# Gate and up projections of a feed-forward as seven products of half-size blocks

## What is computed

```python
def swiglu(x, w_in, w_out):
    g, u = jnp.split(x @ w_in, 2, axis=-1)
    return (jax.nn.silu(g) * u) @ w_out
...
        f = swiglu(rms_norm(h, norm_pre_ffn[layer]), w_ffn_in[layer], w_ffn_out[layer])
        h = h + rms_norm(f, norm_post_ffn[layer])
```

## Time and profile before

| | us |
|---|---|
| median of 3 runs | 1938.16 |
| span of the profiled execution | 1936.8 |
| TensorE busy | 1895.3 |
| VectorE busy | 1025.4 |
| ACT busy | 774.5 |
| last feed-forward after its first four tiles, to L1466 | 341.4 |

### The profile page before, as it was taken

One profiled execution on the slowest core, in us unless ns is written; L12 is line 12 of the kernel. 1 busy time (PEld: TensorE's weight loads), 2 busy tenths in 40 slices (PEclk: granted clock), 3 DMA queues, 4 the chain that ended last, 5 costly groups with the idle time before them and its releaser, 6 DMA issues.

```text
span 1936.8 us, 28778 instructions
## 1 busy us (share of the span) xinstructions
PE 1895.3 (98%) x11544; PEld 1664.7 (86%) x11544; DVE 1025.4 (53%) x1465; ACT 774.5 (40%) x1259; POOL 32.2 (2%) x31
## 2 busy tenths in 40 slices
PE   7999999999999999999999999999999999999997
PEld 7888789999999999888888877787899888888886
DVE  4654475654444455544444467778547463333335
ACT  5355443433222345423232434635675442212232
POOL 0100000100000000000000000000000000000000
PEclk9999999999999999999999999999999999999998
DMA  5111101232222222322222222222103122232221
GB/s 190 68 66 45 58 1 57 87 103 88 95 91 88 92 95 88 109 98 92 93 98 98 91 95 87 76 76 77 55 1 116 70 98 90 86 101 103 89 92 50
DMA packets 47187, 162.36 MB, mean 84 GB/s; under 512 B 5368, under 2 KB 7672, under 8 KB 46936
## 3 DMA queue, kind: packets, MB, share of 16 engines
q1 hardware_dynamic: 46208, 158.60, 23.8%
q10 hardware_dynamic: 856, 2.00, 0.3%
HBM read 156.38 MB, written 4.19 MB: 83 GB/s over the span
## 4 chain that ended last, share of the span: by engine, by line
PE 94%; DVE 3%; ACT 2%; DVEq 1%; issue 1%; DMA 0%; SPq 0%; ACTq 0%
PE ps L468 80%; PE ps L1048 2%; PE ps L919 1%; PE ps L589 1%; PE ps L1068 1%; PE ps L895 1%; PE ps L897 1%; PE ps L1053 0%; PE ps L992 0%; PE ps L564 0%; DVE wlo L2364 0%; ACT WU L2065 0%; PE ps L565 0%; PE ps L1180 0%; PE ps L1209 0%
## 5 line engine op out<-in xcount | busy, mean ns | idle before, releaser
L468 PE MATMUL ps<-UH,whi 128*128 128x264 f32 (+2 forms) x1904 | 646.2, 339 | 13.5 <-DVE wlo L2364 10.2
L468 PE MATMUL ps<-UL,whi 128*128 128x264 f32 (+2 forms) x1904 | 637.6, 335 | 0.0
L468 PE MATMUL ps<-UH,wlo 128*128 128x264 f32 (+3 forms) x1616 | 522.0, 323 | 0.0
L1529 ACT ACTIVATE whi<-raw 128x1024 fp32r<-128x1024 f32 x282 | 295.7, 1052 | 436.3 <-PE ps L468 415.5
L468 PEld LDWEIGHTS ps<-UH,whi 128*128 128x128 f32 x1904 | 358.6, 188 | 55.3 <-issue 13.6
L468 PEld LDWEIGHTS ps<-UL,whi 128*128 128x128 f32 x1904 | 358.6, 188 | 39.5 <-issue 2.4
L2364 DVE TENSOR_TENSOR wlo<-raw,whi 128x1024 fp32r<-128x1024 f32 x248 | 308.3, 1246 | 48.7 <-ACT whi L1529 37.0
L468 PEld LDWEIGHTS ps<-UH,wlo 128*128 128x128 f32 (+1 forms) x1616 | 303.8, 188 | 24.6
L468 PE MATMUL ps<-HH,whi 128*128 128x264 f32 (+1 forms) x768 | 246.4, 321 | 0.0
L468 PE MATMUL ps<-HL,whi 128*128 128x264 f32 (+1 forms) x768 | 246.3, 321 | 0.0
L468 PE MATMUL ps<-HH,wlo 128*128 128x264 f32 (+1 forms) x768 | 245.7, 320 | 0.0
(11 more groups left out here) (466 smaller groups left out, 2358.5 us busy)
## 6 DMA issues: line engine op xcount, KB each, us to landing
raw<-W SPq DMA_DIRECT2D x284, 512.0 KB, 3.2
H<-xT SPq DMA_DIRECT2D x4, 528.0 KB, 7.3
spill<-H SPq DMA_DIRECT2D x1, 2048.0 KB, 9.0
H<-spill SPq DMA_DIRECT2D x1, 2048.0 KB, 8.6
MEM<-memT ACTq DMA_DIRECT2D x1, 1024.0 KB, 4.7
out<-H SPq DMA_DIRECT2D x2, 512.0 KB, 3.0
out<-H SPq DMA_DIRECT2D x4, 256.0 KB, 3.1
masks<-masks SPq DMA_DIRECT2D x1, 768.0 KB, 10.1
```

Source lines behind the costliest of these rows:

```text
L468: mm = pe.matmul(dst, a, b, start=start and n == 0, stop=stop_ and n == 2)
L1529: act.activation(whi[s % NB][:, :, :], raw[s % NB][:, :, :], ACT.Copy).then_inc(w_hi, 1)
```

## The change

Of the 22 pairs, 4 stay as they are (PLAIN) and 18 are computed by seven products instead of eight (the Winograd form of Strassen's scheme). A pair is seen as a 2 x 2 matrix of weight blocks (gate or up by the first or second four of the 8 feature blocks) times a 2 x 2 matrix of token blocks (the same two groups of four by tokens 0 to 255 or 256 to 511). Each product has 4 blocks, three passes and 256 tokens.

- *Token parts.* Seven combinations of the normed input, each 4 x 256 per partition, are made once: VectorE scales the tokens by gain and norm factor (`tokens`, XQ), makes four sums, ACT rounds (`tokens_hi`, TH), VectorE subtracts (`tokens_lo`, TL). So gate and up tiles of these pairs carry the norm's factor.
- *Weight parts.* Four sums of weight blocks per pair are made by VectorE (`pair_sums`, PS), then rounded and subtracted like a slot. A pair has four slots: three of 8 blocks, one of 4.
- *Accumulators.* Bank x collects b11, t2, t3, t4; ACT copies it after b11, after t2 and after t3 (`shot`, snap), and bank z after t1, before b22 is added to it; y holds b21. VectorE builds gate and up halves from banks and copies. Pairs take banks 4, 5, 6 and 7, 1, 3 in turn.
- *Down projection.* Instead of two rounds of 11 groups: four chunks of 4 groups, each in four pieces of two tiles (`down(c, q)`), two pieces before pair 0 and one behind each of pairs 0, 1 and 4 to 15, and a last round of 6 groups. Each is added to FO in memory.
- *Plain pairs* 2 and 3 go to banks 4, 5, 0 and 2, the first of them behind r_ready 7.
- *SP* loads the two slots of a pair as one DMA of 1 MB (`refill_pair`), a down slot as one of 512 KB (`refill_down`).

TensorE:

```diff
+            def plain(bank, *free):
+                pe.wait_ge(*free)
+                for k in range(KT):
+                    wh, wl = take()
+                    mm = passes(ps[:, bank, :], wh, wl, UH[:, k, META:L], UL[:, k, META:L], k == 0, k == KT - 1)
+                mm.then_inc(tile_done, 1)
...
+            def product(bank, v, half, t, first):
+                for k in range(4):
+                    mm = passes(ps[:, bank, 0:NMEM], whi[v % NB][:, 4 * half + k, :], wlo[v % NB][:, 4 * half + k, :],
+                                TH[:, t, k, :], TL[:, t, k, :], first and k == 0, k == 3, True)
+                mm.then_inc(AFTER["pair"][0], 1)
...
+                if i >= 2:
+                    pe.wait_ge(*later("pair_out", 4 * (i - 2) + 4))
+                pe.wait_ge(w_lo, v + 1)
+                turned_in(1)
+                product(x, v, 0, b11, True)
+                turned_in(2)
+                product(y, v, 1, b21, True)
+                pe.wait_ge(w_lo, v + 2)
+                turned_in(4)
+                pe.wait_ge(*later("snap", 4 * i + 1))
+                product(x, v + 1, 0, t2, False)
+                turned_in(5)
+                product(z, v + 1, 1, t1, True)
+                pe.wait_ge(w_lo, v + 3)
+                turned_in(6)
+                pe.wait_ge(*later("snap", 4 * i + 2))
+                product(x, v + 2, 0, t3, False)
+                pe.wait_ge(*later("snap", 4 * i + 3))
+                product(z, v + 2, 1, b22, False)
+                pe.wait_ge(w_lo, v + 4)
+                turned_in(7)
+                pe.wait_ge(*later("snap", 4 * i + 4))
+                product(x, v + 3, 0, t4, False)
+            first = TILE0["ffn"]
+            plain(4, r_ready, 7)
+            plain(5, r_ready, 7)
+            plain(0, evac[0], first // 2 + 1 + FREE)
+            plain(2, evac[1], first // 2 + 1 + FREE)
+            down(0, 0, EARLY_SLOT)
+            down(0, 1, EARLY_SLOT + 1)
+            for i in range(PAIRS):
+                pair(i)
+                if i in DOWN_AFTER:
+                    down(*DOWN_AFTER[i], DOWN_AT[i])
```

ACT, the start and a pair (next_hi is the down slot's high part first, where there is one, then the next pair's):

```diff
+            def shot(i, n, bank, done, kept):
+                act.wait_ge(*later("pair", 7 * i + done))
+                if i:
+                    act.wait_ge(*later("pair_out", 4 * (i - 1) + kept))
+                act.activation(snap[:, n, :], ps[:, bank, 0:NMEM], ACT.Copy).then_inc(AFTER["snap"][0], 1)
+            plain_silu(0)
+            plain_silu(1)
+            weights_hi(0, to=FFN_SLOT + 7)
+            f_hi(0)
+            weights_hi(0, to=FFN_SLOT + 8)
+            f_hi(1)
+            tokens_hi(b11, 0, 1)
+            plain_silu(2)
+            tokens_hi(t1, 0, 2)
+            weights_hi(0, to=FFN_SLOT + 9)
+            tokens_hi(b21, 2, 3)
+            tokens_hi(b22, 3, 3)
+            f_hi(2)
+            weights_hi(0, to=FFN_SLOT + 10)
+            tokens_hi(t3, 1, 4)
+            plain_silu(3)
+            pair_hi(0, 0)
+            f_hi(3)
+            tokens_hi(t2, 3, 5)
+            tokens_hi(t4, 2, 6)
+            for q in range(1, 4):
+                pair_hi(0, q)
...
+                shot(i, 0, x, 1, 1)
+                next_hi(i, 0)
+                shot(i, 1, x, 3, 3)
+                shot(i, 2, z, 4, 2)
+                next_hi(i, 1)
+                shot(i, 3, x, 5, 2)
+                next_hi(i, 2)
+                act.wait_ge(*later("pair_out", 4 * i + 3))
+                act.activation(GA[i % 2][:, :], GA[i % 2][:, :], ACT.Silu).then_inc(N["f_silu"], 1)
+                next_hi(i, 3)
+                f_hi(PLAIN + i)
+                if i in DOWN_AFTER:
+                    next_hi(i, 4)
```

VectorE, from the first gate to pair 0, then a pair, then the half evictions of the end (`tokens` is one instruction of 512 elements, `tokens_lo` one of 1024):

```diff
+            gate(0, first, 0)
+            gate(1, first + 2, 1)
+            gated_up(0, first + 1, 2)
+            gated_up(1, first + 3, 3)
+            weights_lo(0, to=FFN_SLOT + 7)
+            weights_lo(0, to=FFN_SLOT + 8)
+            f_lo(0)
+            f_lo(1)
+            for k in range(4):
+                x = tokens(k)
+            x.then_inc(AFTER["t_x"][0], 1)
+            gate(2, first + 4, 4)
+            tokens_lo(b11, 0, 1)
+            dve.drain()
+            dve.tensor_tensor(XQ[:, 0, :, :], XQ[:, 0, :, :], XQ[:, 1, :, :], ALU.subtract).then_inc(AFTER["t_x"][0], 1)
+            for k in range(4, KT):
+                x = tokens(k)
+            x.then_inc(AFTER["t_x"][0], 1)
+            gated_up(2, first + 5, 5)
+            dve.drain()
+            dve.tensor_tensor(XQ[:, 1, :, :], XQ[:, 3, :, :], XQ[:, 1, :, :], ALU.subtract).then_inc(AFTER["t_x"][0], 1)
+            weights_lo(0, to=FFN_SLOT + 9)
+            tokens_lo(b21, 2, 3)
+            tokens_lo(b22, 3, 4)
+            gate(3, first + 6, 0)
+            weights_lo(0, to=FFN_SLOT + 10)
+            f_lo(2)
+            gated_up(3, first + 7, 2)
+            dve.drain()
+            dve.scalar_tensor_tensor(XQ[:, 3, :, :], XQ[:, 3, :, :], -1.0, XQ[:, 0, :, :], ALU.mult, ALU.subtract
+                                     ).then_inc(AFTER["t_x"][0], 1)
+            f_lo(3)
+            dve.scalar_tensor_tensor(XQ[:, 2, :, :], XQ[:, 3, :, :], -1.0, XQ[:, 2, :, :], ALU.mult, ALU.subtract
+                                     ).then_inc(AFTER["t_x"][0], 1)
+            down_out(0, 0)
+            pair_sums(0)
+            down_out(0, 1)
+            pair_lo(0, 0)
+            tokens_lo(t2, 3, 6)
+            down_out(0, 2)
+            tokens_lo(t1, 0, 2)
+            pair_lo(0, 1)
+            down_out(0, 3)
+            tokens_lo(t3, 1, 5)
+            pair_lo(0, 2)
+            tokens_lo(t4, 2, 7)
+            pair_lo(0, 3)
...
+                dve.wait_ge(*later("pair", 7 * i + 2))
+                dve.wait_ge(*later("snap", 4 * i + 1))
+                dve.tensor_tensor(a[:, 0:NMEM], ps[:, y, 0:NMEM], snap[:, 0, :], ALU.add).then_inc(AFTER["pair_out"][0], 1)
+                if i in DOWN_AFTER:
+                    down_lo(i)
+                if i + 1 < PAIRS:
+                    pair_sums(i + 1)
+                next_lo(i, 0)
+                dve.wait_ge(*later("snap", 4 * i + 4))
+                dve.tensor_tensor(c[:, NMEM:SEQ], snap[:, 3, :], snap[:, 2, :], ALU.add).then_inc(AFTER["pair_out"][0], 1)
+                dve.wait_ge(*later("pair", 7 * i + 6))
+                dve.tensor_tensor(a[:, NMEM:SEQ], ps[:, z, 0:NMEM], snap[:, 1, :], ALU.add).then_inc(AFTER["pair_out"][0], 1)
+                next_lo(i, 1)
+                dve.wait_ge(*later("pair", 7 * i + 7))
+                dve.wait_ge(N["f_silu"], j + 1)
+                dve.scalar_tensor_tensor(c[:, 0:NMEM], ps[:, x, 0:NMEM], -1.0, a[:, 0:NMEM], ALU.mult, ALU.mult
+                                         ).then_inc(AFTER["pair_out"][0], 1)
+                dve.drain()
+                dve.scalar_tensor_tensor(c[:, NMEM:SEQ], c[:, NMEM:SEQ], -1.0, a[:, NMEM:SEQ], ALU.mult, ALU.mult
+                                         ).then_inc(AFTER["f_c"][0], 1)
+                next_lo(i, 2)
+                if i in DOWN_AFTER:
+                    down_out(DOWN_AFTER[i][0], 2 * DOWN_AFTER[i][1])
+                f_lo(j)
+                if i in DOWN_AFTER:
+                    down_out(DOWN_AFTER[i][0], 2 * DOWN_AFTER[i][1] + 1)
+                next_lo(i, 3)
...
             def evict_half(x, e):
-                a = GA[e][:, part(x)]
+                o = FO[:, KT - 2 + e, x * NMEM:(x + 1) * NMEM]
                 dve.wait_ge(tile_done, t + 2 * x + e + 1)
-                dve.drain()
-                dve.tensor_tensor(a, ps[:, 2 * ((t + e) % 2) + x, 0:NMEM], R[0][:, part(x)], ALU.mult)
-                dve.drain()
-                o = FO[:, KT - 2 + e, part(x)]
-                dve.tensor_tensor(o, o, a, ALU.add).then_inc(h_final, 1)
+                dve.tensor_tensor(o, o, ps[:, 2 * ((t + e) % 2) + x, 0:NMEM], ALU.add).then_inc(h_final, 1)
```

SP:

```diff
+            def refill_pair(i, ready):
+                s = PAIR_SLOT + 2 * i
+                sp.wait_ge(w_lo, ready)
+                sp.dma_start(raw_p[i % 2][:, :, :].rearrange("p (a s) e -> p a (s e)", a=2),
+                             W[s:s + 2].rearrange("a p s e -> p a (s e)")).then_inc(AFTER["pair_in%d" % (i % 2)][0], 16)
...
+            for i in range(PAIRS):
+                if i + 2 < PAIRS:
+                    refill_pair(i + 2, PAIR_AT[i] + 4)
...
+                if i in DOWN_AFTER and i != DOWN_ORDER[-1]:
+                    sp.wait_ge(w_lo, DOWN_AT[i] + 1)
+                    refill_down(DOWN_ORDER.index(i) + 1)
```

More of the change, by code:

```diff
@@ L94 @@
 END_OF = tile_ends()
-assert len(END_OF) == _t and END_OF[-1] == NBLOCKS
+assert len(END_OF) == _t and END_OF[-1] <= NBLOCKS
 def last_tile(slot):
@@ new lines, in down @@
+            def down(c, q, v):
+                pe.wait_ge(w_lo, v + 1)
+                for x in range(2):
+                    t = DOWN_TILE + KT * c + 2 * q + x
+                    pe.wait_ge(evac[t % 2], t // 2 + FREE)
+                    for k in range(CHUNK):
+                        f = CHUNK * c + k
+                        if q == 0 and x == 0:
```

(4 more changed lines are left out.)

350 lines of the change are left out of this document (256 added, 94 removed).

## The result

The changed kernel takes 1908.6 us (median of 4 executions: 1906.97, 1907.21, 1909.99 and 1916.27), the kernel before on the same chip 1938.19 us (4 executions, 1937.76 to 1938.74). The profiled execution is the slowest of the four, 1916.27 us with a span of 1914.5 us. That one lies on the forecast of 1916.4; the other three do not. So there are two questions: did each step come as forecast in the profiled execution, and what do the other three have that it has not.

A forecast was written before the change was run, and what follows sets the result against it. TensorE was taken to bound the kernel. Matmuls -19.1, start gap -2.5, clock -1.7, stalls +2.6 and tail -1.0 sum to -21.7 us, from the median 1938.16 to 1916.4 us; range 1912 to 1923.

The forecast's parts named there:

- What bounds the kernel: Whole kernel: TensorE, busy 98% of the span, sets the time; only matmul time or a TensorE stall can be won.
- Part 1: Eighteen gate/up pairs: seven half-width products replace eight, at 0.118 us per narrow matmul; L1466 is reached 19.1 us earlier.
- the low end: Bottom of the forecast range, 1912 us: no stall at all and 0.117 us per narrow matmul.
- the walk: The three engines' instruction lists laid side by side in order, priced with trace durations, to find when TensorE must wait.
- Part 2: Start of the last feed-forward: the 2.35 us bank-wait gap goes, 2.5 us won, and its half clock, 1.7 us.
- Part 3: ACT and VectorE readiness: 2.6 us of stalls, 2.1 at block 3 of the first down piece, 0.5 in the pairs.
- Part 4: Tail behind L1466: two half evictions on the chain become an add alone, 0.5 us each, 1.0 us won.
- 1, the stall halves the clock: Rival: the new 2.1 us stall at the start halves the clock behind it, 1.7 us more, 1918.1 us; chance 0.22.
- 2, VectorE behind all through: Rival: VectorE durations 10% longer in start and bare pairs, 4.8 us more stall, 1921.2 us; chance 0.15.
- 3, snapshots: Rival: TensorE waits in every pair for ACT's accumulator copies, making the kernel slower than before; chance 0.05.
- 4, narrow matmuls not at half the time: Rival: narrow matmuls take 0.1325 us, so seven products win nothing, about 1938 us; chance 0.03.

The follow-up runs named there:

- eight: Changed kernel with the product of b21 made twice in each of the 18 pairs, 12 narrow matmuls more per pair; 1939.93 us, ratio 1.0006.
- gap: Changed kernel with the first plain tile waiting again for the eviction of an early tile, as before the change; 1916.36 us, ratio 0.9875.
- again2: Changed kernel run once more without any edit, to see how its executions spread; 1912.15 us, ratio 0.9873.
- again: Changed kernel run once more, unmodified, beside the first variants; 1917.89 us, ratio 0.9891.
- again3: Changed kernel run unmodified on the same chip as the last variant, for comparison; 1912.48 us, ratio 0.986.
- restart: Changed kernel with TensorE waiting ahead of each down piece behind a pair until VectorE has built that pair's last tile, 14 times; 1946.31 us, ratio 1.0039.
- kick: Changed kernel with one extra matmul of 130 tokens, result unused, in front of the second product of pair 9; 1913.42 us, ratio 0.9868.
- kickall: Changed kernel with f_lo(3) ahead of the token sum and an extra 130-token matmul in all 18 pairs; 1911.02 us, ratio 0.9862.
- best: Changed kernel with f_lo(3) ahead of the token sum and an extra 130-token matmul in pairs 0 and 4 only; 1909.45 us, ratio 0.9851.
- flo: Changed kernel with the low part f_lo(3) moved ahead of the token sum that stood before it; 1910.18 us, ratio 0.9861.
- flo2: Second run, without further edit, of the changed kernel with f_lo(3) ahead of the token sum; 1910.53 us, ratio 0.9864.
- kicksizes: Changed kernel with one extra matmul in each of pairs 4 to 13, of lengths from 64 to 256 tokens; 1910.81 us in one execution.

## Why the prediction was right and wrong

**What bounds the kernel**: right. 216 narrow matmuls more made the span 25.0 us longer (**eight**), and a gap of 0.93 us of idle 1.2 us longer (**gap**).

**Part 1, seven for eight, -19.1 us**: the failed step. The count is right, the price of the narrow matmul is not: 0.118 us was taken as its one price, and the pairs ran at 0.1178 us in some executions and at 0.1134 in others. "I take 0.2318 and 0.118 (the second from the tail [...])" took one price for the narrow matmul from two stretches that happened to have it, and the low end went to 0.117 only. The trace of the kernel before had a third stretch of narrow matmuls, in the projection of the mixer, where they start 0.113 us apart. Its timeline on TensorE:

```profile
1486.58 0.28 PE L468 MATMUL ps<-YH,whi 128*128 128x256 f32 x1
...
1489.41 0.28 PE L468 MATMUL ps<-YL,whi 128*128 128x256 f32 x1
```

From the first to the last row 25 matmuls later it is 2.83 us. I did not look there. (This stretch is at 0.1136 us in all 14 traces, whatever the pace of the pairs: it shows the lower price, not that one stretch can have either.) With 0.1134 for the 1512 narrow matmuls of the pairs the term is 7.0 us larger, 26.1 us. By this row the low end, which takes no stall, is 1916.4 - 2.6 - 7.0 = 1906.8, and the median of 1908.6 lies inside. In the profiled execution, of the slower pace, the term came out: 321.58 us from the first plain matmul to L1634, stall included, where the walk gave 320.4 + 2.6 = 323.0. The wide matmuls took 0.2332 us instead of 0.2318, 0.8 us in 588.

**Part 2, the start, -2.5 and -1.7 us**: the gap went, as the timeline shows. The price of the clock is not borne out. The trace of the kernel before has two stretches of half clock ahead of the tail, one behind the gap and one near 1445 us; the kernel after has two as well, near 742 and 1445 us, both ahead of the stretch of the change; **again2** has one, near 1422 us. Over the executions the mean granted clock is 0.9954 for the 38 of the kernel before and 0.9954 for the 17 of the changed one. A loss of 1.7 us avoided would raise the mean by 0.0009. So what was won behind the gap was, on average, lost in another place, or these stretches have little to do with the gap. No run here put the old gap back in full (**gap** had 0.93 us), so this stays open.

**Part 3, stalls, +2.6 us**: right in place and too large. The one stall is where the walk had it, at block 3 of the first down piece on f_lo(3), and cost 0.95 us instead of 2.1. f_lo(3) ended 27.5 us behind the first gate step (1570.41 to 1597.92) where the walk had 28.6: the durations agree, but instructions that don't depend on each other overlap a little on VectorE (one of 0.69 us starts at 1592.48 and the next at 1593.09), where I had put 0.05 us between them. In the pairs there is no stall at all, not even in the bare ones, where I had 0.5 us. Transfers were never waited for.

**Part 4, the tail, -1.0 us**: 1.4 us (21.6 to 20.2).

**Sum.** At full clock the change is worth 22.0 us in the slower group; my terms without that of the clock give 20.0, and with the stall as measured 21.7. In the faster group 6.9 us come on top. That the forecast's 21.7 agrees with the slower group is in part luck: 1.7 us for the clock, which the mean clocks don't show, made up for 1.65 us too much of stall. The forecast of 1916.4 was the time of the slower group, and 7 of the 17 executions belong to the other, among them three of the four that made the result.

**Rivals.** *1, the stall halves the clock:* it did not, the clock is 1.00 behind it. The bracket in which the rival stood, clock kept behind 1.37 us and lost behind 2.35 us, came from one trace and does not hold. At the place of the earlier trace rows the idle time is 1.11 us in all 14 traces, and in seven of them (**again**, **again3**, **gap**, **eight**, **restart**, **kick**, **kickall**) the clock fell 0.3 to 0.7 us behind it. **again** there, timeline and the window of the low clock:

```profile
236.22 0.27 PE L772 MATMUL ps<-MF,LML 64*128 64x64 f32 x1
237.60 0.47 PE L655 MATMUL ps<-MF,LTH 128*128 128x512 f32 x1 [1.11 <-ACT XE L1862]
```

```profile
238.03:241.44 3.41, 3.41 (x13) 2.27 (x12) 1.48 (x11) 1.97 (x4) 0.00 (x0) 0.50 0.00 0
```

The length of a gap alone does not say whether the clock falls. In the pairs of **restart** the clock fell at the end of the gap of 3.3 us and 1.3 us behind one of 1.81; behind the twelve others of 1.54 to 1.82 us it stayed. The section of the Trainium skill named there (TensorE: Matmul & The Clock Gate, A second HAM failure mode: psum-queue depth-cycling) says that many short idles between groups of matmuls can make the clock swing. **restart** bears this out in small part only: two falls in 14 waits. *2, VectorE behind all through:* ruled out by 1215 ns and by no stall in any bare pair. *3, snapshots:* ruled out, no wait of TensorE has ACT behind it from the first pair to the last. *4, narrow matmuls not at half the time:* the opposite; 0.1178 is 50.5% of 0.2332 and 0.1134 is 48.6%. The section of the Trainium skill cited in part 1 (TensorE: Matmul & The Clock Gate, Back-to-back issue gap) has 81 ns at 128 columns and 131 at 512; the trace does not agree, with 233 at 512.

## What to carry to other kernels

A price that carries the largest term is to be read in every stretch of the trace where such an instruction stands, and the range has to go to the lowest and the highest of them: 4% of the price of 1512 matmuls was worth more than all stalls together. When the times of one kernel fall in two groups, multiply each span by its mean clock and compare the traces of one of each: the count of matmuls in windows of equal length finds a change of pace that no gap, wait or clock shows. Work that adds over a hundred us of VectorE and ACT time costs nothing as long as each instruction is laid against TensorE's list, and the one place where it did cost was the one that the list had shown.

## What was not expected of the hardware

- A dense stream of 256-token matmuls, each with a weight load, has two paces at one granted clock: starts 0.1178 or 0.1134 us apart. In undisturbed executions the pace holds through all 18 pairs (256 us in the kernel after), with 24 wide matmuls between most of them, and can change behind the 108 wide matmuls ahead of the last tiles. It changed at interruptions of 1.5 us and more (**restart**), and was switched by a single matmul of 130 tokens (**kick**). In the slower one the weight loads of one of the three passes take 192 ns instead of 188. Why there are two, and what sets the pace at the start of the stretch, is open.
- Stretches of half clock (granted clock 0.50, 1.2 GHz), 3.4 us each, come ahead of the tail in some executions and not in others. The one near 742 us lies on dense 256-token matmuls behind small products of the mixer, those near 1422 and 1445 us on small matmuls, and TensorE was not idle ahead of them; the one near 238 us comes behind 1.11 us of idle. Seven of the 14 traces have those near 238 and 743 us, the kernel after those near 742 and 1445, the kernel before one near 1444 (and that at the old gap), **again2** and **best** one near 1420 or 1444, and **flo**, **flo2** and **kicksizes** none. Each costs up to 1.7 us, and the executions of one group differ by about what none to two of them make.
